# RWKV chunks: modulation weights in four pieces over the whole weight ring, then both slots of the gates' weights; low parts of the first up projection on GpSimd

## The reference, cut to what matters

```python
# RWKV-7: a recurrence over the 512 tokens, 8 heads of 64
def step(S, inp):
    r_t, w_t, k_t, v_t, kk_t, a_t = inp
    sa = jnp.einsum('bhvk,bhk->bhv', S, -kk_t)
    S = (S * w_t[:, :, None, :] + sa[..., None] * (kk_t * a_t)[:, :, None, :]
         + v_t[..., None] * k_t[:, :, None, :])
    return S, jnp.einsum('bhvk,bhk->bhv', S, r_t)
...
# modulation of both layers of the second block: ada_w is (2, 1024, 6144)
mod_l = (jax.nn.silu(c) @ ada_w[i] + ada_b[i])[:, None, :]
mod_c = (jax.nn.silu(c_ctx) @ ada_w[i] + ada_b[i])[None, None, :]
...
# the gates of the first block, after the mixers' projections
gates = jax.nn.sigmoid(p_gate).reshape(B, L, N_BRANCH, D_MODEL)
...
# the first block's feed-forward layer; D_FF = 2816, CONV_W = 3
def conv_ffn(h, w_up, conv_w, conv_b, w_down):
    u = h @ w_up                      # (512, 1024) @ (1024, 5632): the first up projection
    u = lax.conv_general_dilated(...) + conv_b
    gate, val = jnp.split(u, 2, axis=-1)
    return (jax.nn.silu(gate) * val) @ w_down
```

## Time and profile before

| | |
|---|---|
| timed runs | 3898.07, 3899.34, 3904.71 us |
| profiled execution, its own time | 3900.96 us |
| its span, first to last instruction | 3898.9 us |
| granted TensorE clock over the span, mean | 0.915 of full speed |
| TensorE busy | 3349.1 us |
| VectorE / ScalarE / GpSimd busy | 1635.9 / 1125.3 / 497.3 us |
| chunk stage of RWKV | about 172 to 388 us of the span |
| first up projection | about 1409 to 1697 us of the span |

### The profile page before, as it was taken

One profiled execution on the slowest core, in us unless ns is written; L12 is line 12 of the kernel. 1 busy time (PEld: TensorE's weight loads), 2 busy tenths in 40 slices (PEclk: granted clock), 3 DMA queues, 4 the chain that ended last, 5 costly groups with the idle time before them and its releaser, 6 DMA issues. The chain is left out here.

```text
span 3898.9 us, 49072 instructions
## 1 busy us (share of the span) xinstructions
PE 3349.1 (86%) x19354; PEld 2484.8 (64%) x19354; DVE 1635.9 (42%) x2526; ACT 1125.3 (29%) x1694; POOL 497.3 (13%) x366
## 2 busy tenths in 40 slices
PE   7688856797698889988868788999996999989998
PEld 5365521365455567766747667888654888847877
DVE  5433359522222457743155533222002788724332
ACT  2311323221311232223255533222002455413321
POOL 0000035000000110003302212000002222200001
PEclk9799877896599999999989888999998999989999
DMA  3266110121023112212100001111111111212222
GB/s 131 94 239 238 44 46 1 37 76 41 1 86 119 44 65 86 86 62 100 44 27 1 1 22 44 65 65 58 45 60 55 70 62 66 76 65 78 95 81 81
DMA packets 30423, 268.43 MB, mean 69 GB/s; under 512 B 2848, under 2 KB 5280, under 8 KB 10144
## 3 DMA queue, kind: packets, MB, share of 16 engines
q1 hardware_dynamic: 30240, 265.88, 18.9%
HBM read 261.68 MB, written 4.19 MB: 68 GB/s over the span
## 5 line engine op out<-in xcount | busy, mean ns | idle before, releaser
L595 PE MATMUL banks<-normed_high,weights_high 128*128 128x512 f32 (+1 forms) x2272 | 856.0, 377 | 145.2 <-DVEq L547 91.3
L595 PE MATMUL banks<-normed_low,weights_high 128*128 128x512 f32 (+1 forms) x2272 | 846.2, 372 | 0.0
L595 PE MATMUL banks<-normed_high,weights_low 128*128 128x512 f32 (+1 forms) x2272 | 845.1, 372 | 0.0
L595 PEld LDWEIGHTS banks<-normed_high,weights_high 128*128 128x128 f32 x2272 | 436.6, 192 | 256.4 <-DVEq L547 107.2
L261 DVE TENSOR_TENSOR weights_low<-ring,weights_high 128x1024 fp32r<-128x1024 f32 (+1 forms) x239 | 324.0, 1356 | 653.8 <-ACTq L534 633.5
L532 ACT ACTIVATE weights_high<-ring 128x1024 fp32r<-128x1024 f32 (+1 forms) x239 | 278.3, 1164 | 804.5 <-PE banks L595 500.0
L595 PEld LDWEIGHTS banks<-normed_high,weights_low 128*128 128x128 f32 x2272 | 436.9, 192 | 74.1
L595 PEld LDWEIGHTS banks<-normed_low,weights_high 128*128 128x128 f32 x2272 | 437.6, 193 | 69.1
L564 POOL TENSOR_TENSOR latent_total<-latent_total,latent_square 128x512 f32<-128x512 f32 x42 | 77.1, 1837 | 1880.9 <-ACTq L517 1880.9
L595 PE MATMUL banks<-ffn_hidden,ring 128*128 128x256 f32 (+1 forms) x704 | 227.3, 486 | 1.1 <-PEq L152 1.1
L2788 PE MATMUL banks<-normed_high,hg_weights_high 128*128 128x512 f32 (+1 forms) x512 | 187.1, 366 | 30.4 <-POOL hg_weights_low L2749 30.4
(11 more groups left out here) (514 smaller groups left out, 4958.8 us busy)
## 6 DMA issues: line engine op xcount, KB each, us to landing
ring<-in_ffn_up SPq DMA_DIRECT2D x33, 2048.0 KB, 8.1
ring<-in_ada SPq DMA_DIRECT2D x48, 1024.0 KB, 5.1
ring<-in_ffn_down SPq DMA_DIRECT2D x24, 1408.0 KB, 6.0
ring<-in_hgrn SPq DMA_DIRECT2D x16, 1536.0 KB, 6.5
ring<-in_gates SPq DMA_DIRECT2D x6, 2048.0 KB, 8.0
ring<-in_wo SPq DMA_DIRECT2D x6, 2048.0 KB, 8.2
ring<-in_w_rw SPq DMA_DIRECT2D x4, 2048.0 KB, 10.7
ring<-in_branch SPq DMA_DIRECT2D x3, 2048.0 KB, 8.0
```

What stands on the lines that cost most here:

```text
L595: mm = pe.matmul(ps[:, 0:y.shape[-1]], w, y, start=(kk == 0 and n == 0), stop=(kk == kt - 1 and n == len(pairs) - 1))
```

## The change

The modulation groups get four places, two in each half of the ring, and four semaphores. `ada_load` puts group n into half (n // 2) % 2, column block n % 2. Four groups are issued in `rwkv_gates`, and in `rwkv_chunks` group n is issued when the product of group n - 4 is done. The ring's first half is no longer free for the first slot of `gates0`: `w_rw` is called with `keep_free=2`, and both slots of `gates0` are loaded at the end of the chunks. Apart from that, `linear` gets an argument `low_on`; the first up projection passes "gpsimd", so that its weights' low parts are computed in a loop of GpSimd and no longer by VectorE. The products, their order on TensorE and everything else stay.

```diff
--- before.py
+++ after.py
@@ -461,7 +461,7 @@
 
 
 def linear(k, section, parts, evac, nslots=None, kt=DT, tiles=4, on="vector", per=1, beside=None, more=None,
-           weights_move=False, keep_free=0, sums=(), norms=(), fetch=None):
+           weights_move=False, keep_free=0, sums=(), norms=(), fetch=None, low_on="vector"):
 
 
 
@@ -606,13 +606,13 @@
             def emptier(name):
                 def run(eng):
                     e = k.engine(eng, name + "_steps", ends)
-                    steps = len(parts) * sum(p for p, o in zip(per, on) if o == name) + (tiles if split else 0)
+                    prepare = {"scalar": high, low_on: low}.get(name) if split else None
+                    steps = len(parts) * sum(p for p, o in zip(per, on) if o == name) + (tiles if prepare else 0)
                     if name == "scalar" and beside is not None:
                         steps += beside[1]
-                    prepare = high if name == "scalar" else low
                     if sums and name == "scalar":
                         eng.preload_act_table_set("natural_log_exp_and_others")
-                    if split:
+                    if prepare:
                         prepare(e, (0, None, 0))
                     if norms and name == "scalar":
                         scalar_norms(k, e, norms, summed)
@@ -621,7 +621,7 @@
                             r.by_scaler(e)
                     for s, i in lay.walk(lambda: e.loop(lay.rounds, lay.body * steps)):
                         for j, ahead in lay.tiles_ahead(s, i):
-                            if ahead is not None and split:
+                            if ahead is not None and prepare:
                                 prepare(e, ahead)
                             if sums and name == "scalar" and s * tiles + j:
                                 squares(e, s * tiles + j - 1)
@@ -639,8 +639,10 @@
                         squares(e, DT - 1)
                     ends[name + "_steps"] = e.n - k.count(name + "_steps").base
                 return run
-            if "vector" in on or split:
+            if "vector" in on or split and low_on == "vector":
                 block.vector(emptier("vector"))
+            if split and low_on == "gpsimd":
+                block.gpsimd(emptier("gpsimd"))
             if "scalar" in on or split or beside is not None or sums or norms:
                 block.scalar(emptier("scalar"))
             if split:
@@ -875,7 +877,7 @@
                                            ALU.mult, ALU.add).then_inc(e.sem, e.tick())
                 e.eng.wait_ge(e.sem, e.now())
 
-            linear(k, "w_rw", [k.H.operand(LAT)], shift, per=2, keep_free=1, norms=[lead])
+            linear(k, "w_rw", [k.H.operand(LAT)], shift, per=2, keep_free=2, norms=[lead])
         with ExitStack() as s1:
             CW = k.sb("silu_c_window", [P, DT, ADA_QUADS, 32], s1)
             rwkv_gates(k, PR, A, G, KK, LD, GKD, CW)
@@ -885,8 +887,8 @@
 
 def ada_load(k, sp, n):
 
-    half, c = (k.place["gates0"] + 1) % 2, (n % 2) * 4 * ADA_WIDE
-    sp.dma_start(k.ring[:, half, c:c + 4 * ADA_WIDE], k.dram["ada"][n]).then_inc(k.count(f"ada_loaded_{n % 2}").sem, 16)
+    half, c = n // 2 % 2, (n % 2) * 4 * ADA_WIDE
+    sp.dma_start(k.ring[:, half, c:c + 4 * ADA_WIDE], k.dram["ada"][n]).then_inc(k.count(f"ada_loaded_{n % 4}").sem, 16)
 
 
 def rwkv_gates(k, PR, A, G, KK, LD, GKD, CW):
@@ -901,7 +903,7 @@
             @block.sync
             def _(sp):
                 sp.dma_start(WS[:], k.dram["rw_up"]).then_inc(fetched.sem, 16)
-                for n in range(2):
+                for n in range(4):
                     ada_load(k, sp, n)
 
             @block.gpsimd
@@ -1041,8 +1043,7 @@
         FW = N
         banks = k.PS
         ada_used, ada_moved = k.count("ada_used"), k.count("ada_moved")
-        ada_loaded = [k.count(f"ada_loaded_{x}") for x in range(2)]
-        ada_half = (k.place["gates0"] + 1) % 2
+        ada_loaded = [k.count(f"ada_loaded_{x}") for x in range(4)]
         ADA = banks[7]
         NONE = k.sb("no_rows", [P, P], s)
         nothing = k.count("no_rows_cleared")
@@ -1061,11 +1062,12 @@
         with k.stage() as (block, ends):
             @block.sync
             def _(sp):
-                for n in range(2, ADA_GROUPS):
-                    sp.wait_ge(ada_used.sem, ada_used.at(n))
+                for n in range(4, ADA_GROUPS):
+                    sp.wait_ge(ada_used.sem, ada_used.at(n - 2))
                     ada_load(k, sp, n)
                 sp.wait_ge(ada_used.sem, ada_used.at(ADA_GROUPS + 1))
-                k.load_slot(sp, k.place["gates0"] + 1)
+                for g in range(2):
+                    k.load_slot(sp, k.place["gates0"] + g)
 
             @block.gpsimd
             def _(g):
@@ -1122,11 +1124,11 @@
                 def modulate(i, q):
 
                     m = i * ADA_QUADS + q
-                    pe.wait_ge(ada_loaded[m % 2].sem, ada_loaded[m % 2].at(16 * (m // 2 + 1)))
+                    pe.wait_ge(ada_loaded[m % 4].sem, ada_loaded[m % 4].at(16 * (m // 4 + 1)))
                     for j in range(4):
                         c = ((m % 2) * 4 + j) * ADA_WIDE
                         mm = pe.matmul(ADA[32 * j:32 * j + 32, :], CW[:, i, q, :],
-                                       k.ring[:, ada_half, c:c + ADA_WIDE], start=False, stop=False)
+                                       k.ring[:, m // 2 % 2, c:c + ADA_WIDE], start=False, stop=False)
                     mm.then_inc(ada_used.sem, 1)
 
                 def group(dst, terms):
@@ -1313,7 +1315,7 @@
                 ends["vector_steps"] = e.n - k.dve_steps.base
             ends.update(products_ready=len(PRODUCTS), operands_ready=len(VECTOR), moved_by_scalar=len(SCALAR),
                         ada_used=2 + ADA_GROUPS, ada_moved=1, no_rows_cleared=1,
-                        ada_loaded_0=8 * ADA_GROUPS, ada_loaded_1=8 * ADA_GROUPS)
+                        **{f"ada_loaded_{x}": 4 * ADA_GROUPS for x in range(4)})
 
 
 def rwkv_out(k, PR, G, Y):
@@ -2146,7 +2148,7 @@
                     e.eng.wait_ge(e.sem, e.now())
                     e.eng.sem_inc(squashed.sem, 1)
             linear(k, "ffn_up", [H.operand(LAT)], conv, per=[3, 3, 6, 6], beside=(silu, 2),
-                   more={"squashed": FT}, norms=[lead])
+                   more={"squashed": FT}, norms=[lead], low_on="gpsimd")
         residual_linear(k, "ffn_down", U.operand(LAT), kt=FT, tiles=1, sums=[
             Squares("latent", lambda t: X[:, t, LAT], L, 4),
             Squares("regained", lambda t: X[:, t, LAT], L, 5, scale=lambda t: k.root_gain[:, t:t + 1])])
```

## The result

The changed kernel takes 3855.59 us, the median of four runs (3851.75 to 3858.17); the kernel before, on the same chip, 3899.52 (3898.07 to 3904.71). The ratio is 0.9884, with 95% interval 0.9871 to 0.9896. The profiled execution took 3853.15 us with a span of 3850.8; the forecast was 3850 with a range of 3840 to 3868. Two later series of the same kernel gave 3855.95 and 3856.45. From one profiled execution to the other the gain is 47.8 us, from median to median 44 to 46.

A forecast was written before the change was run, and what follows sets the result against it. TensorE, busy for 86% of the span, was taken to bound the kernel, so only its waits pay. Chunk stage -23.0 and first up projection -26.5 gave -49.5 us, from 3899.34 to 3850 us, range 3840 to 3868.

The forecast's parts named there:

- The landings: RWKV chunk stage: four modulation pieces instead of two end all TensorE waits for their loads, -23.0 us.
- VectorE's second place: Wait before a chunk's sixth product: VectorE's scaling and copy might become late there; some 0.1 us to spare.
- The two small terms: Chunk stage: less low clock (0 to 3.4 us gained) against more issue stops (up to 11 lost); 2 each, cancelling.
- part 1: RWKV chunk stage with four modulation pieces instead of two: -23.0 us, bounds -12 to -27.
- "issue" far over 3 us: Sign in the chunk stage: TensorE stops without a shown cause, 3.0 us before, growing far more would prove rival (a).
- rival (a): Chunk stage: issue stops or VectorE take over the landing waits, leaving 12 of 23 us, 3861 us; chance 0.12.
- The gates' loads: End of the chunks: two gate weight loads issued there land before ScalarE reads the first; costs nothing, at most 8.5 us.
- The slots: First up projection: low parts on GpSimd bring ten slots from 24.63 to 21.76 us each, -28.7 us.
- The first slot: First up projection: GpSimd delays the norm by 1.0 us and low part 1 by 1.2; +2.2 us (0 to 5).
- part 2: First up projection with its weights' low parts on GpSimd: -28.7 + 2.2 = -26.5 us, bounds -20 to -29.

The follow-up runs named there:

- quarters: The changed kernel with each 1 MB modulation piece loaded by four DMAs of 512 columns: 3866.54 us, ratio 0.9908.
- small loads: The changed kernel with each modulation load cut to 64 of 2048 columns, 32 KB instead of 1 MB (result not the reference's): 3841.40 us, ratio 0.9855.

## Why the prediction was right

**The landings (taken -23.0): right.** All 23.0 us of waits went, none moved to VectorE's second place, and the load had room: 6.7 us of 9.0. The 0.1 us that the forecast saw to spare at the second place does not follow from its figures: VectorE's copy would end at 320.51 + 0.42 = 320.93 and the product at 321.4, which leaves 0.5.

**The two small terms (taken as 2 each, to cancel): direction right, both sized too small.** Issue stops grew by 7.1 us (10.1 - 3.0), within the bound of 11, and nearer to it than to the 2 taken. TensorE's busy time fell by 5.7 us over the whole stage, from 186.3 to 180.6, with the time at low clock going from 20.5 us to 3.4. The bound had been 3.4 because only two stretches of 9 us were read, in the first chunk and the second, and not all of the stage: its longest time at low clock, 13.7 us from 371.8 on, lies at the end. The terms cancel to 1.4 us all the same, and part 1 is 219.1 - 196.8 = 22.3 us. That the total came out so near was luck: two errors of opposite sign. By the forecast's own sign ("issue" far over 3 us) rival (a) holds, and its mechanism did appear, though it took 7.1 us and not 12 and the clock gave most of it back. The argument that the sum gave for more stops, a denser stage, does not make them by itself.

**What a stop is.** In the trace each of the 11 stops ends 1.3 to 1.5 us after the end of a 16 KB packet of the instruction queue, and so do the 5 of before and all 13 with quarters (worked out from the packets' times). About such a packet, the stretch from 274 to 278 us, with the stop that ends at 277.99 (queue, packets, MB, share of 16 engines; then the first product after it):

```profile
q1 hardware_dynamic: 110, 0.77, 46.2%
q8 instruction: 1, 0.02, 1.4%
```

```profile
277.99 0.51 PE L1141 MATMUL banks<-rwc_inv,rwc_n2t 64*64 64x64 f32 x11 [2.09 <-issue]
```

The packet takes 1.4% of 64 us, 0.90; its median over the stage is 0.95 to 1.00 us in all these kernels, stops or none. So the transfer itself isn't slowed. It starts too late, and that can be counted: every kernel has 33 such packets in the stage, and the traces tell at which of TensorE's matmul records each one starts. With small loads the packets come at about even steps, the fourth to the eighth at records 437, 564, 695, 808 and 954 of the stage. In the changed kernel the same five start at 526, 620, 763, 848 and 1012. Over all 33, packets start later than with small loads by 21 records in the mean with one load in flight, 25 in the kernel before, 35 with a limit of two, 42 to 45 with three or four, and 55 with quarters. The stops go with them: 2.8, 3.0, 4.6 to 6.8, 10.1 to 10.9 and 16.9 us, and 0 with small loads. An estimate from chunks of 21.73 us and 529 records: 42 records are 1.7 us.

So loads in flight delay the fetches of TensorE's instructions. Where a fetch stands in line no record shows, and neither whether it is the number of loads or where they fall in time that counts: each limit changes both. With one load in flight the stage is also slower (249.2 us), so that fewer stops there have two reasons. The Trainium skill ("Advanced Engine Details and Errata", section "ISA Cache") gives lines of 256 instructions. The trace agrees: the stage has 4232 matmul and 4232 weight-load records, and 8464 in 33 packets are 256 each.

**The gates' loads (taken 0): right,** landed by 370 for a use at 395.

**The slots (taken -28.7): right,** 245.9 - 217.6 = 28.3 us in every kernel with the edit as it is. The low part took 2.40 us against 2.48 taken. VectorE's multiplication was stretched from 0.69 us to 0.97 in the median and 1.26 at most, less than the forecast's 1.6, and free, as said. The Trainium skill ("SBUF — State Buffer", section "Who interferes with whom") says that a VectorE instruction with two SBUF inputs contends with a GpSimd one that reads SBUF, and counts casts among those that can. The traces agree on both: with two low parts in a row the cast, which has one input, was stretched from 0.43 to 2.54 us.

**The first slot (taken +2.2): right in the waits,** which grew by 1.4 + 1.1 = 2.5 us, the 1.0 and 1.2 of the forecast. The time grew by 0.2 in the one execution and by 3.1 in others; in the first, the time at low clock in slot 0 was 6.8 us, before it 6.8 and 3.4; in the executions with 3.1 it was 13.7 and 23.9. The bound -20 of part 2 is wider than its working gives: -28.7 + 5 is -23.7.

**The remainder.** 22.3 + 28.3 - 0.2 is 50.4 us; the profiled executions differ by 47.8, and what lacks is mostly the 3.1 us of the untouched stages in between. The median lies 2.4 us above the profiled execution, where the one before lay 1.6 under it: together that is why 3850 became 3855.6.

## What to carry to other kernels

In a stage whose instructions are fetched as it runs, try keeping no more data in flight than hides the landing: here a limit of two loads of 1 MB gave 3849.17 and 3850.24 us, a limit of four 3855.95 and 3856.45, and one load 3906.57. Buffer places and loads in flight are two sizes, and may be set apart with one more wait on the queue's engine. An operation moved to GpSimd can cost VectorE time too: here its multiplication and cast in SBUF stood until GpSimd's low part was through, while its operations from PSUM did not. So weigh it against what VectorE, and whoever waits for VectorE, has free, not only against its own deadline.

## What was not expected of the hardware

Cutting 1 MB loads into 256 KB ones, with no more bytes in flight, raised the stops from 10.4 to 16.9 us; the stage then has four times as many packets, and why they cost more is not shown. And the stages between the chunks and ffn_up took between 995.1 and 1001.8 us in executions of the same instructions, with 324 to 338 us of them at low clock: a difference of 7 us between two single profiles shows nothing by itself.
